# Scaling the attention probabilities inside their transposition: a product with a diagonal matrix in place of two elementwise passes and a transpose

## The reference

```
qg  = q * Dh**-0.5                                  # 16 heads, 4 key/value heads, Dh = 64
p_c = masked_softmax(qg @ kc.T - slope * d_c)       # compressed keys
p_s = masked_softmax(qg @ k_s.T - slope * d_s)      # selected blocks
p_w = masked_softmax(qg @ kw.T - slope * d_w)       # window
o   = g0 * (p_c @ vc) + g1 * (p_s @ v_s) + g2 * (p_w @ vw)
```

## Time and profile before

| | |
|---|---|
| median of 3 runs | 1832.52 us (1831.91 to 1833.79) |
| the profiled execution | 1833.2 us |
| its span, first to last instruction | 1831.4 us |
| TensorE busy | 1711.1 us, 93% of the span |
| VectorE, ScalarE, GpSimd busy | 652.5, 522.6, 148.6 us |
| mean granted TensorE clock | 0.979 |
| first and last transpose of the prompt's probabilities | 1275.8 and 1409.1 us |

### The profile page before, as it was taken

The page is one execution under the profiler, slowest core; times in us unless marked ns, Lnnn a source line. Parts: engine busy times, 40 slices in busy tenths (PEclk is TensorE's granted clock), DMA queues, the critical chain, the costliest instruction groups (busy, mean ns, idle before and its releaser), DMA issues.

```text
span 1831.4 us, 53901 instructions
## 1 busy us (share of the span) xinstructions
PE 1711.1 (93%) x23793; PEld 1370.3 (75%) x23793; DVE 652.5 (36%) x1686; ACT 522.6 (29%) x1341; POOL 148.6 (8%) x219
## 2 busy tenths in 40 slices
PE   5999999999998898999999899999999989999996
PEld 3877777777776585999987764587776777999984
DVE  4341116777775333111112400313886241111114
ACT  3112213333332113111112210313998131111113
POOL 2111100000000002000001000000332002000002
PEclk8999999999999998999999899998999999999998
DMA  8666845334344488999997895265000388999944
GB/s 320 208 226 206 267 131 183 108 107 119 119 121 143 150 251 319 415 416 417 418 369 226 195 242 155 105 154 139 2 2 3 90 348 345 416 413 420 417 176 175
DMA packets 195433, 413.66 MB, mean 226 GB/s; under 512 B 53702, under 2 KB 135330, under 8 KB 186722
## 3 DMA queue, kind: packets, MB, share of 16 engines
q1 hardware_dynamic: 176434, 358.08, 56.7%
q0 software_dynamic: 11040, 39.85, 6.0%
q10 hardware_dynamic: 7760, 12.79, 1.9%
HBM read 356.97 MB, written 57.91 MB: 227 GB/s over the span
## 4 chain that ended last, share of the span: by engine, by line
PE 43%; issue 7%; ACT 5%; DMA 3%; DVE 3%; POOL 1%; DVEq 0%; ACTq 0%; SPq 0%; POOLq 0%
PE bank L2088 12%; PE bank L2083 6%; PE bank L2101 5%; PE bank L2107 4%; PE bank L1792 3%; PE bank L2990 3%; PE bank L3137 1%; ACT region_a L3238 1%; ACT region_a L3248 1%; DMA region_b<-in_cmp_w_dram 1%; POOL x_slots L1913 1%; PE bank L3101 1%; PE bank L2193 1%; PE bank L2918 1%; PE bank L2075 1%
## 5 line engine op out<-in xcount | busy, mean ns | idle before, releaser
L2083 PE MATMUL bank<-wg,slot_x 128*32 128x384 f32 x1056 | 119.0, 491 | 2.4 <-ACT slot_x L2282 2.4
L2101 PE MATMUL bank<-wd,actT 128*32 128x384 f32 x1056 | 117.5, 486 | 3.7 <-ACT actT L2301 3.7
L2088 PE MATMUL bank<-wg,slot_x 128*32 128x128 f32 x1056 | 120.4, 275 | 0.0
L2088 PE MATMUL bank<-wu,slot_x 128*32 128x128 f32 x1056 | 119.4, 273 | 0.0
L2088 PEld LDWEIGHTS bank<-wg,slot_x 128*32 128x32 f32 x1056 | 116.2, 111 | 2.6
L2107 PE MATMUL bank<-wd,actT 128*32 128x256 f32 (+1 forms) x704 | 118.0, 326 | 0.0
L2083 PE MATMUL bank<-wu,slot_x 128*32 128x384 f32 x1056 | 118.0, 488 | 0.0
L649 PE MATMUL bank<-xm,wp 128*128 128x272 f32 x480 | 113.8, 396 | 0.4 <-DMA wp<-in_rwkv_w_rkv_dram 0.4
L2088 PEld LDWEIGHTS bank<-wu,slot_x 128*32 128x32 f32 x1056 | 113.5, 110 | 0.0
L649 PEld LDWEIGHTS bank<-xm,wp 128*128 128x128 f32 x480 | 90.4, 190 | 21.3 <-issue 2.7
L2309 ACT ACTIVATE ys<-bank 128x384 f32<-128x384 f32 x32 | 15.7, 490 | 275.8 <-PE bank L2107 275.8
(11 more groups left out here) (672 smaller groups left out, 3976.7 us busy)
## 6 DMA issues: line engine op xcount, KB each, us to landing
wg<-in_moe_w_gate_dram SPq DMA_DIRECT2D x22, 2048.0 KB, 17.1
wu<-in_moe_w_up_dram SPq DMA_DIRECT2D x22, 2048.0 KB, 17.3
wd<-in_moe_w_down_dram SPq DMA_DIRECT2D x22, 2048.0 KB, 17.8
xT<-in_ada_w_dram SPq DMA_DIRECT2D x40, 1024.0 KB, 5.3
w<-in_moe_w_gate_dram SPq DMA_DIRECT2D x10, 2048.0 KB, 16.7
fT<-in_moe_w_up_dram SPq DMA_DIRECT2D x10, 2048.0 KB, 16.7
gall<-in_moe_w_down_dram SPq DMA_DIRECT2D x10, 2048.0 KB, 17.5
wp<-in_rwkv_w_rkv_dram SPq DMA_DIRECT2D x24, 512.0 KB, 4.2
```

The lines of the kernel that those rows point to most:

```text
L2083: mm = pe.matmul(ps[32 * j:32 * j + 32, 0:GW], x[:, k, 32 * j:32 * j + 32], w[:, k, 0:GW], start=k == 0, stop=k == KT - 1)
L2088: mm = pe.matmul(ps[96:128, q * 128:(q + 1) * 128], x[:, kk, 32 * q:32 * q + 32], w[:, kk, GW:FF], start=kk == 0, stop=kk == KT - 1)
L2101: mm = pe.matmul(bank[4 + b][32 * j:32 * j + 32, 0:384], act_piece(k, j), w[:, k, b * 384:(b + 1) * 384], start=k == 0, stop=k == 3)
```

## The change

The probabilities stay as the exponential leaves them. For each unit and half VectorE makes a 64-column matrix in each row half instead: the identity, whose rows are multiplied by the reciprocal sum and the gate of that row. TensorE then multiplies the block of probabilities (stationary, as before) with this diagonal matrix (moving, in place of the identity), by `matmul` and no longer by `transpose`: the result is the transposed and scaled block. GpSimd has no part in it any more. The scale matrices and the identity's two halves lie in the sample tokens' key columns of `kvtok`, and so VectorE first waits for the stores of these.

```diff
@@ main program, POOL
             pool_moe(pool, B, 0, regs)
-            pool_attend(pool, B)
             pool_moe(pool, B, 1, regs)
@@ allocate_nsa
+    B.scales = [B.kvtok[:, 4, 128 * i:128 * i + 128].rearrange("p (h n) -> p h n", h=2) for i in range(NSC)]
+    B.id_halves = B.kvtok[:, 4, 512:576]
@@ pe_attend, turn(u)
-        pe.wait_ge(S("side_rows"), KT + u + 1)
         if u >= 1:
             pe.wait_ge(S("pt_ev"), 2 * u)
...
-                    mm = pe.transpose(bank[4 + r][:, at:at + 64], B.sc[u % NSC][hs(r), h, kt * 128:(kt + 1) * 128], ident[hs(r), hs(r)])
+                    mm = pe.matmul(bank[4 + r][:, at:at + 64], B.sc[u % NSC][hs(r), h, kt * 128:(kt + 1) * 128], B.scales[u % NSC][hs(r), h], start=True, stop=True)
@@ normalise(eng, B, u, h)
-    v, g = B.sc[u % NSC][:, h, 0:128 * (i + 1)], 3 * heads(j)[h] + 1 + br
-    return eng.tensor_scalar(v, v, B.sm[u % NSC][:, h:h + 1], B.gates[:, i, g:g + 1], ALU.mult, ALU.mult)
-
-
-def pool_attend(pool, B):
-    S = B.sem
-    for u in range(NU):
-        pool.wait_ge(S("dve_rows"), KT + u + 2)
-        normalise(pool, B, u, 1).then_inc(S("side_rows"), 1)
+    g = 3 * heads(j)[h] + 1 + br
+    return eng.tensor_scalar(B.scales[u % NSC][:, h], B.id_halves, B.sm[u % NSC][:, h:h + 1], B.gates[:, i, g:g + 1], ALU.mult, ALU.mult)
@@ dve_attend
     dve.wait_ge(S("stored"), 48)
+    dve.wait_ge(S("kv_stored"), 16 * 11)
+    dve.tensor_tensor(B.id_halves, B.ident[:, 0:64], B.ident[:, 64:128], ALU.add)
     dve.memset(B.scc_flat, 0.0)
...
-            dve.reciprocal(sm, sm).then_inc(S("dve_rows"), 1)
+            dve.reciprocal(sm, sm)
             dve.drain()
-            normalise(dve, B, u, 0).then_inc(S("p_ready"), 1)
+            normalise(dve, B, u, 0)
+            normalise(dve, B, u, 1).then_inc(S("p_ready"), 1)
```

## The result

The changed kernel takes 1885.84 us (median of 4 runs, 1881.40 to 1887.36) against 1833.15 for the kernel before (now 4 runs, 1831.91 to 1837.09): ratio 1.0276, 95% interval 1.0258 to 1.0295. I had forecast 1864, within 1850 to 1880: the side was right, the size was not.

The account below looks back on a forecast made before the run. TensorE was to become the bound: a head pair's 14.2 us of work, plus 4.9 for products and 1.1 of waits, makes 20.3 us, 3.9 more; eight pairs add 31.4 to 1832.5, giving 1864 us, range 1850 to 1880.

Parts of the forecast that it names:

- What bounds the kernel now: Attention loop: TensorE and ScalarE both near full, busy 15.28 and 15.47 us of a 16.36 us head pair.
- the free 2.1: TensorE's waits in a head pair, 2.1 us of 16.36, which added work was to fill at no cost.
- What is removed, what is added on VectorE: Scaling in 64 units: GpSimd's removed work worth nothing; VectorE's two scalings add 1.4 us a head pair, less than TensorE needs.
- What is changed on TensorE: Turns' 80 transposes become products at 101 ns instead of 40: 8.1 us for 3.17, 4.9 more a head pair.
- the 3.17 us of before: Eight turns of a head pair in the kernel before, timed start to start: 3.17 us, 40 ns a transpose.
- What of it is hidden: TensorE's waits in a head pair shrink from 2.1 to 1.1 us, since turns still wait for ScalarE's copies.
- Base and sum: Median 1832.5 us plus 31.4 for eight head pairs, each growing 3.9 to 20.3 us, gives 1864 us.
- Load and product in series: Rival for the turns: load and product cannot overlap in one half, 160 ns a product, 1902 us; chance 0.07.
- The factor of four: Skill's statement that transpose mode is four times faster for FP32, giving an estimate of 160 ns a product.
- The other side: Rival for the turns: a diagonal product costs what a transpose costs, gain at most 7.1 us, 1826 us; chance 0.05.
- The range's upper end: No wait vanishes in the loop: +39.4 us, +42 with 53 ns an instruction, 1875 us, opened by 5 to 1880.

Follow-up runs that it names:

- e6: Kernel before, with ordinary products with the identity in the turns of query tiles 0 and 1 only: 1850.82 us, ratio 1.0056 to the kernel before.
- e7: Kernel before, with ordinary products with the identity in the turns of query tile 3 only: 1853.68 us, ratio 1.0081 to the kernel before.
- e1: Changed kernel with the transpose back, leaving the blocks unscaled while VectorE still makes the scale matrices: 1889.12 us, ratio 1.0292 to the kernel before; head pair 16.41 us.
- e2: Kernel before with only the turn's transpose replaced by an ordinary product with the identity, scaling left as it was: 1885.81 us, ratio 1.0268 to the kernel before.
- e3: Changed kernel with 32 moving columns instead of 64 in each product of the turn: 1910.99 us, ratio 1.0403 to the kernel before.
- e4: Changed kernel with all products of one row half, then all of the other, instead of alternating: 1972.49 us, ratio 1.0727 to the kernel before.
- e12: Changed kernel with each turn's products made twice, the second over the first: 1955.84 us, 70.0 above the changed kernel; head pair 31.16 us.
- e8: Changed kernel run once more without an edit, beside the kernel before: 1891.61 us, ratio 1.0275 to the kernel before.
- e10: Changed kernel with whole f32 products of 128x128 instead of two halves: 1880.57 us, ratio 1.0260 to the kernel before.

## Why the prediction was wrong, point by point

- **What bounds the kernel now.** Right as to the two engines. Wrong in "the free 2.1 is what the edit may fill at no cost": e6 and e7 added 1.9 and 2.6 us of work and the head pair grew by 1.7 and 2.6. I had counted waits as room; they are links of one chain with ScalarE's copies and exponentials.
- **What is removed, what is added on VectorE.** Right. VectorE has 14.80 us in a head pair (forecast 14.6), a scaling takes 312 ns (310), the add 0.22 us under cover, GpSimd's work was worth nothing (e1, e2).
- **What is changed on TensorE.** The mechanism was right: two instructions for a product, 188 ns loads, a pace that doesn't depend on the columns (e3), two halves side by side (e4). This is the step that failed, by its size: "51 ns each, 101 ns a product", 8.1 us. The runs showed 56 ns (e12) and 0.6 us of boundaries, 9.57 us: 1.5 us a head pair, 12 us for eight. The row was of the right shape but in a place with a head start. The pitch of its loads stood beside it and was the better figure, but I miscounted it: 53 ns where seven steps of pairs give 56. And the boundaries had been in the 3.17 us of before without a counterpart in the sum of after: transposes start 32 ns apart inside a block, (0.57 - 0.22)/11 in the x12 of the earlier trace rows, which makes 2.6 us for 80 and leaves 0.6. With 56 ns and these 0.6 I would have had 9.56.
- **What of it is hidden.** 1.1 us of waits were forecast, 1.7 are read off the blocks. The periods give the surer figure: TensorE's work grew by 9.57 - 3.17 = 6.4 us and the head pair by 5.85, so 0.55 us was hidden, not 1.0; that is 0.45 us a head pair, 3.6 us for eight. Ahead of tile 1's second turn and tile 0's first I had counted the signal one way only. ScalarE's copies also begin late behind the turn that they wait for, 0.16 us after 1353.01 and 0.26 after 1367.68:

```profile
1353.17 0.66 ACT L3238 ACTIVATE kvtok<-bank 128x256 f32<-128x256 f32 x2 [0.77 <-PE bank L3101]
...
1367.94 1.08 ACT L3238 ACTIVATE region_a<-bank 128x512 f32<-128x512 f32 x2 [1.80 <-PE bank L3101]
```

  So 0.26 and 0.41 us stayed there, where I had 0.15 and 0.2. Ahead of tile 3's first turn, where I had counted both ways, 0.63 stayed for 0.55.
- **Base and sum.** Forecast 3.9 a head pair, measured 5.85; the two terms above make 20.3 + 1.5 + 0.45 = 22.25 of 22.21. Eight pairs are 46.8 us; the loop's 48.6 has 1.8 more, in the filling and at the loop's start, where the clock was 0.85 from 1280 to 1300 and 0.99 before. The last 4 us of the 52.7 lie outside the loop, where e2 (47.6 us in all) shows none. e2 itself took 1885.81 us, the changed kernel 1885.84; what differs is the kernel before, 1838.2 beside the one and 1833.15 beside the other. So these 4 us are scatter, as far as this tells.
- **The rivals.** Load and product in series is out for the alternating halves: 56 ns, not 80. The factor of four that I weighed with it (the Trainium skill, TensorE: Matmul & The Clock Gate, section Terms) gave an estimate of 160 ns; the trace shows 120, three times the transpose's 40. The other side is out by e2, and its 7 us by e1. The range's upper end, 42 us over the base plus 5, took every wait as staying and still fell short, because its price was short: 8 x 6.4 = 51 us in place of 42.

## What to carry to other kernels

A product by a diagonal in f32 is no free ride on a transpose: here 120 ns against 40 for the same block, and of the versions run only those in bf16 paid, by 0.3 to 0.5%. Before pricing a block by its neighbour's, take the pitch of its weight loads, look whether they come singly or in pairs, and count the boundaries where the shape of the stationary operand changes. And an engine's waits are not room by themselves: ask of each wait what starts the work that it waits for, and whether it would shrink if this engine came later. In the chain of two engines here it did not.

## What the runs showed of the hardware that was not expected

- The granted clock from 1280 to 1300 us, at the start of the same loop, was 0.50 in one run and 0.85 in another of the same kernel (e8 and the first profile). In the 12 us before, TensorE had been busy for 9.32 us in both, at a clock of 0.77 and 0.69. The loop that began at 0.50 took 11 us more. With 32 moving columns instead of 64 (e3), or with the halves in turn (e4), the clock fell as low as 0.50 and stayed below 1.00 for longer, though TensorE was busy nearly throughout. What decides it was not tested.
- One pace holds for three forms of the f32 product: instructions start 112 ns apart in one row half with 64 moving columns (e4), 112 in the full array with 128 moving columns (e10), and 56 with two halves alternating (e12).
